# A recurrence's filler products cut into smaller parts, and vector steps put in another order, in a two-block transformer kernel

## The chip, the core and the metric

The kernel runs on one core of a Trainium2 chip. The core has a matrix engine (TensorE, in the rows PE, with PEld for its weight loads), a vector engine (VectorE, DVE), a scalar engine (ScalarE, ACT), GpSimd (POOL) and SyncE (SP, here the one that streams weights in). The engines run their own instruction lists and wait for one another through semaphores. The metric is the device time of one execution in microseconds, lower is better.

## What is computed

The reference runs two blocks over 512 tokens of 1024 values in float32. The change touches the first block; its mixer holds the recurrence (HGRN2, four heads of 128 keys, both directions) around which most of the change lies:

```python
def forget(z, lb):
    f = lb + (1.0 - lb) * jax.nn.sigmoid(z.astype(f32))
    return ((1.0 - f)..., jnp.log(f)...)
k_f, lf_f = forget(fz_f, lb_fwd)
k_b, lf_b = forget(fz_b, lb_bwd)
o_f = gla_chunkwise(qh, k_f, lf_f, vh)           # S_t = diag(f_t) S_{t-1} + k_t v_t^T, o_t = S_t^T q_t
o_b = gla_chunkwise(qh[:, ::-1], k_b[:, ::-1], lf_b[:, ::-1], vh[:, ::-1])[:, ::-1]
...
def first_block(...):
        h = h + token_mixers(rms_norm(h, norm_mix[l]), ...)
        h = h + memory_cross_attention(rms_norm(h, norm_mem[l]), rms_norm(mem, norm_mem_kv[l]), ...)
        h = h + conv_ffn(rms_norm(h, norm_ffn[l]), ...)
    return rms_norm(h, final_norm)
```

The second block (two attentions, with a top-k selection) is left as it was.

## The kernel before

**Products.** Every float32 product is made of three matmuls on rounded halves: high times high (line 621), low times high (622), high times low (623). A group of the three is called a *triple* here; a projection of 128 output columns over 1024 inputs is 8 triples of 512 columns. Weights come as slots of 128x1024 from one long stream: SyncE loads a slot into `ring` (2 deep), GpSimd splits it into `wH` and `wL` (3 deep; lines 573, 574, 576), and signals `split_done`. TensorE opens slots in stream order, so the list `STREAM` and the order of the products must agree. Products land in two PSUM banks in turn (slot number modulo 2), and a bank is opened again when the engine that reads it has freed it.

**The recurrence.** A head has four tiles of 128 tokens (`ST`). For each head h, TensorE turns the logarithms of the forget gates (`turn_logs`, line 756), sums them to decays between tiles (`cross_decays`, 746 and 747) and inside one (`tile_decays`, 788), which ScalarE exponentiates into `E` (`decays`, 1383). VectorE multiplies `E` by queries and keys into `X` (`tile`, 1933; `cross`, 1887 to 1894), TensorE makes scores of `X` in `pair[3]` (`tile_scores`, 801 to 806), VectorE multiplies them by level masks into `lev` (1942) and adds the levels up into `Sg` (1948); these two together are `select`. `output` (836) takes `Sg` to the values. There is one `lev` and one `pair[3]`: `tile_scores` of a tile waits for the masks of the tile before (`masked`), and the mask waits for the sum of the levels before (`s_made`).

Ahead of head h+1 VectorE makes its gates (`forget`, 1858 and 1859, into `lf`), ScalarE their logarithm (1365), TensorE `turn_logs(h+1)`, ScalarE the high part (`logs_high`, 1369), VectorE the low part (`logs_low`, 1953, into `lftL`), for which `cross_decays(h+1)` waits. `keys` (1864, 1867) scales the keys in place.

**The filler.** Between these dependent steps TensorE projects what comes later: while head h runs, the four products and the value turn of head h+2 (`beside(h, j)`, in heads 2 and 3 the attention's q, k, v and the gate), whole products but for one, which `half_step` cuts into 4 and 4 triples around `tile_scores(h, 3)` and `cross_decays(h+1)`.

**The norms.** After the products `mix_out` and `mem_o`, VectorE takes each of 8 chunks (`residual`, 1823), scales it (`with_gain`, 2229), subtracts ScalarE's rounded high part for `nL` of the chunk before (`low`, 1757), and adds the chunk's square to `sums` (`accumulate`, 1766). The next product reads `nL` chunk by chunk; one matmul over `sums` (606) follows.

The order on each engine is the order in which its block of the program is written.

Of the kernel before, what the change touches and what calls it, by code (L numbers as in the profile page):

```python
# [23 lines left out]
P = 128  # L24
# [40 lines left out]
SPL = 3  # L65
# [13 lines left out]
for _h in (1, 2):  # L79
# [6 lines left out]
    ("head2", [1] * 3 + [0]), ("head3", [1] * 4 + [0]), ("q_a", [1] * 4),  # L86
# [31 lines left out]
def head_at(h, j):  # L118

    if j == 0 and h in (1, 2):  # L120
        return f"forget{h}", 0
    if j == 4 and h < 2:
        return f"turn{h}", 0
    return f"head{h}", j - (h in (1, 2))
# [144 lines left out]
def build(nc, stream, xT, memT, pos, vecs, ident_d, const_r, const_a, const_d, sink_d, relb_d, gvec, x1_d, out_d):  # L269
    with ExitStack() as ctx:  # L270
# [318 lines left out]
        def _(pe):  # L589
# [126 lines left out]
            def half_step(h, half):  # L716

                g = head_slot(h, 3)
                if half == 0:
                    open_bank(g)  # L720
                    open_slot()
                r = (n_slot[0] - 1) % SPL
                for k in range(4 * half, 4 * half + 4):
                    last = three(bank(g % 2), weight(r, k), n_parts[k], k == 0, k == DC - 1)
                if half:
                    last.then_inc(multiplied, 1)
# [15 lines left out]
            def recurrence(beside):  # L742
# [109 lines left out]
                for h in range(HG_HEADS):  # L852
# [6 lines left out]
                    tile_scores(h, 1)  # L859
                    if more:  # L860
                        beside(h, 2)
                    else:
                        project("v_a", 0, 1, n_parts)
# [4 lines left out]
                    if h + 2 < HG_HEADS:  # L868
                        half_step(h + 2, 0)
                    else:  # L870
                        beside(h, 3 if more else 2)
                    tile_scores(h, 3)
                    if more:
                        cross_decays(h + 1)
                    if h + 2 < HG_HEADS:
                        half_step(h + 2, 1)
                    if not more:
                        beside(h, 3)
                    if more:
                        tile_decays(h + 1, 0)  # L880
                    beside(h, 4)
                    if more:
# [133 lines left out]
            def head_beside(h, j):  # L1016
                if h + 2 < HG_HEADS:
                    head_step(h + 2, j)
                elif h + 2 == HG_HEADS and j < 4:
                    project("q_a", j, 1, n_parts)  # L1020
                elif h + 1 == HG_HEADS:
                    if j == 1:
                        project("k_a", 0, 1, n_parts)
                    if j < 2:
                        for c in (2 * j, 2 * j + 1):
                            rotate("first", c, qa[:, c, :], FIRST["q_a"] + c, c_a("perm", 0, P), q_turn(c))
# [238 lines left out]
        def _(act):  # L1265
# [94 lines left out]
            def recurrence(beside):  # L1360
# [52 lines left out]
                for h in range(HG_HEADS):  # L1413
                    n, more = UNITS * h, h + 1 < HG_HEADS
                    cross_copies(h)
                    decays(n + 2, LQ)
                    beside(h, 1)
                    decays(n + 3, LQ)
                    if more:
                        logs(h + 1)  # L1420
                    decays(n + 4, LQ)
                    beside(h, 2)
                    if more:
                        logs_high(h + 1)
# [1218 lines left out]
```

## Time and profile before

| what | value |
|---|---|
| time before, median of 3 runs (range) | 1480.76 us (1479.05 to 1482.13) |
| the profiled execution, its own time | 1481.16 us |
| its span, first to last instruction | 1479.4 us |
| TensorE matmuls busy | 1454.1 us, 98% of the span |
| VectorE / ScalarE / GpSimd busy | 928.5 / 452.5 / 832.8 us |
| mean granted TensorE clock | 0.997 |

The profiled execution's time is 1.76 us more than its span; the sums of the prediction are made against this execution. "Busy" of TensorE counts modelled ends of pipelined matmuls that overlap, so what is left of the span is what it stood still, by a lower bound.

### The profile page before, as it was taken

What the parts mean: (1) busy time and instruction counts of PE and PEld (TensorE: products, weight loads), DVE (VectorE), ACT (ScalarE), POOL (GpSimd) and SP (SyncE); (2) the same over time, 40 slices, a digit from 0 to 9 for tenths busy, and PEclk for the clock granted to TensorE, in tenths of its full rate; (3) what the DMA queues carried; (4) which work ended last, traced back from release to release, by engine and by line L of the source; (5) the groups of instructions that cost most, each with busy time, mean ns of one, the idle gap of its engine ahead of it and who ended that gap; (6) DMA issues with size and microseconds to landing.
All of it is one profiled execution on the core that took longest, in us unless ns stands there. A gap on an engine that the chain in (4) does not pass through costs nothing.

```text
span 1479.4 us, 20094 instructions
## 1 busy us (share of the span) xinstructions
PE 1454.1 (98%) x7044; PEld 1151.7 (78%) x7044; DVE 928.5 (63%) x1685; ACT 452.5 (31%) x889; POOL 832.8 (56%) x675
## 2 busy tenths in 40 slices
PE   9999999999999999999999999999999999999998
PEld 7877777767788888778888888887867677767887
DVE  5577787787238433478777673334877777696245
ACT  4456332376123122320101001112343334464112
POOL 5624313534566777466776767766665354444662
PEclk9999999999999999999999999999999999999999
DMA  5311112121333333233333333334324542323332
GB/s 197 87 57 58 41 31 58 57 61 55 114 100 100 114 101 109 64 99 88 97 100 100 92 94 103 110 100 137 99 72 146 93 104 57 114 72 108 106 93 78
DMA packets 37017, 135.60 MB, mean 92 GB/s; under 512 B 4296, under 2 KB 4552, under 8 KB 36296
## 3 DMA queue, kind: packets, MB, share of 16 engines
q1 hardware_dynamic: 33264, 121.13, 27.3%
q10 hardware_dynamic: 3672, 13.35, 3.5%
q8 instruction: 56, 0.92, 0.2%
q14 instruction: 25, 0.20, 0.0%
HBM read 127.64 MB, written 6.82 MB: 91 GB/s over the span
## 4 chain that ended last, share of the span: by engine, by line
PE 88%; DVE 6%; issue 2%; ACT 2%; PEld 1%; DMA 0%; PEldq 0%; DVEq 0%; ACTq 0%
PE pair L621 25%; PE pair L623 24%; PE pair L622 24%; PE pair L908 4%; PE pair L936 3%; PE pair L920 2%; PE pair L836 1%; PE pair L788 1%; PE pair L801 1%; DVE X L1933 1%; DVE dx L2089 1%; PE pair L705 0%; PE pair L823 0%; DVE selm L2365 0%; DVE dx L2086 0%
## 5 line engine op out<-in xcount | busy, mean ns | idle before, releaser
L576 POOL TENSOR_TENSOR wL<-ring,wH 128x1024 fp32r<-128x1024 f32 x223 | 546.9, 2453 | 18.6
L621 PE MATMUL pair<-nH,wH 128*128 128x512 f32 x1064 | 426.3, 401 | 3.2 <-DVE nL L1757 1.9
L623 PE MATMUL pair<-nH,wL 128*128 128x512 f32 x1064 | 414.9, 390 | 0.0
L622 PE MATMUL pair<-nL,wH 128*128 128x512 f32 x1064 | 414.7, 390 | 0.0
L573 POOL TENSOR_TENSOR tick<-tick 128x1 f32<-128x1 f32 x223 | 57.5, 258 | 604.3 <-PE pair L623 558.0
L621 PEld LDWEIGHTS pair<-nH,wH 128*128 128x128 f32 x1064 | 199.7, 188 | 64.3 <-issue 18.9
L574 POOL TENSOR_SCALAR wH<-ring 128x1024 fp32r<-128x1024 f32 x223 | 237.1, 1063 | 0.0
L623 PEld LDWEIGHTS pair<-nH,wL 128*128 128x128 f32 x1064 | 199.7, 188 | 42.7
L622 PEld LDWEIGHTS pair<-nL,wH 128*128 128x128 f32 x1064 | 199.9, 188 | 41.2 <-issue 1.9
L1600 ACT ACTIVATE sgb<-cv 128x512 f32<-128x512 f32 x22 | 13.9, 634 | 209.5 <-DVE cv L2274 209.5
L621 PE MATMUL pair<-aH,wH 128*128 128x512 f32 x176 | 68.5, 389 | 0.0
L622 PE MATMUL pair<-aL,wH 128*128 128x512 f32 x176 | 68.5, 389 | 0.0
L623 PE MATMUL pair<-aH,wL 128*128 128x512 f32 x176 | 68.5, 389 | 0.0
L1766 DVE TENSOR_TENSOR sums<-sums,sq 128x512 f32<-128x512 f32 (+1 forms) x30 | 53.0, 1766 | 11.7 <-ACT sq L1298 11.0
L1933 DVE TENSOR_TENSOR X<-E,qT 128x128 f32<-128x128 f32 x96 | 31.7, 331 | 44.8 <-ACT E L1383 44.8
L2273 DVE SCALAR_TENSOR_TENSOR cv<-gpad,vec,cv 128x512 f32<-128x512 f32 x22 | 56.7, 2579 | 0.8
L2300 DVE TENSOR_TENSOR hT<-pair,hT 128x512 f32<-128x512 f32 x8 | 5.5, 692 | 77.3 <-PE pair L623 77.3
L1457 ACT ACTIVATE dx<-dx,stat 128x128 f32<-128x128 f32 (+3 forms) x64 | 36.0, 563 | 55.9 <-DVE stat L2095 55.6
L2270 DVE TENSOR_TENSOR gpad<-pair,rstd 128x512 f32<-128x512 f32 x22 | 15.2, 692 | 56.3 <-PE pair L623 56.2
L2107 DVE TENSOR_SCALAR dx<-dx,stat 128x128 f32<-128x128 f32 (+3 forms) x64 | 45.9, 717 | 2.3
L1383 ACT ACTIVATE E<-pair 128x768 f32<-128x768 f32 (+1 forms) x40 | 32.0, 853 | 40.8 <-PE pair L747 23.5
L621 PEld LDWEIGHTS pair<-aH,wH 128*128 128x128 f32 x176 | 33.0, 188 | 6.9
(403 smaller groups left out, 2657.6 us busy)
## 6 DMA issues: line engine op xcount, KB each, us to landing
ring<-stream SPq DMA_DIRECT2D x223, 512.0 KB, 3.6
gvec<-gv ACTq DMA_DIRECT2D x1, 2560.0 KB
hT<-xT SPq DMA_DIRECT2D x4, 512.0 KB, 6.0
x_d<-hT ACTq DMA_DIRECT2D x1, 2048.0 KB, 7.3
toep<-gvec ACTq DMA_DIRECT2D x8, 256.0 KB, 3.3
hT<-x_d ACTq DMA_DIRECT2D x1, 2048.0 KB, 8.6
out<-yo SPq DMA_DIRECT2D x4, 512.0 KB, 3.6
cD<-const_d ACTq DMA_DIRECT2D x1, 1345.0 KB, 6.4
```

What stands on the lines that cost most here:

```text
L573: pool.tensor_tensor(tick[:, 1:2], tick[:, 0:1], tick[:, 0:1], ALU.add).then_inc(high_done, 1)
L574: pool.tensor_scalar(high, ring[:, r, :], 1.0, 0.0, ALU.mult, ALU.add).then_inc(high_done, 1)
L576: pool.tensor_tensor(low, ring[:, r, :], high.bitcast(F32), ALU.subtract).then_inc(split_done, 1)
L621: mm(out, a[0], b[0], start=first, stop=False)
L622: mm(out, a[0], b[1], start=False, stop=False)
L623: return mm(out, a[1], b[0], start=False, stop=last)
L908: last = mm(out, *pairs[t], start=t == 0, stop=t == count - 1)
L936: last = mm(out[rows, qs], w, turned[:, j % 2, t, qs], start=n_t == 0, stop=n_t == len(kind["serves"]) - 1)
L1766: V.tensor_tensor(sums[:, :width], sums[:, :width], sq[:, a % 2, :width], ALU.add).then_inc(sq_added, 1)
L1933: last = V.tensor_tensor(out, factors(kind), src, ALU.mult)
L2107: V.tensor_scalar(px, px, st[:, 5:6], None, ALU.mult).then_inc(a_prob, 1)
L2273: own(V.scalar_tensor_tensor(out=y, in0=x[:, 0:S], scalar=w[0], in1=y, op0=ALU.mult, op1=ALU.add))
```

## The change

It has four parts. (1) TensorE's filler is cut at triples: `beside_part(h, j, a, b)` issues triples a to b of a product. In heads 0 and 1 the groups between recurrence steps were 8, 8, 4, 4, 8 triples and are 8, 6, 6, 2, 4, 6; in head 2 they were 8, 8, 8 and are 8, 6, 5, 2, 3. The first product of the next head (`forget3`, `q_first`) begins before the value turn, so the stream's order changes there. (2) VectorE makes the gates and scaled keys of head h+1 before tile 1 of head h (for head 0 the scaled keys directly behind its gates), and ScalarE takes their logarithm behind the exponentials of tile 1. (3) `select` is cut into `masks` and `levels`, and the masks of tile 1 go ahead of the products of tile 2. (4) In the two residual norms, the low part of the last chunk goes ahead of the last addition to `sums`, and an addition is made before the next chunk's product is taken.

```diff
@@ -83,7 +83,7 @@
     ("head0", [1] * 4), ("forget1", [1]), ("turn0", [0]), ("head1", [1] * 3), ("forget2", [1]), ("turn1", [0]),
-    ("head2", [1] * 3 + [0]), ("head3", [1] * 4 + [0]), ("q_a", [1] * 4),
+    ("head2", [1] * 3), ("forget3", [1]), ("turn2", [0]), ("head3", [1] * 3), ("q_first", [1]), ("turn3", [0]), ("q_a", [1] * 3),
     ("q_turn", [0] * 2), ("k_a", [1]), ("q_turn2", [0] * 2), ("v_a", [1]), ("g_first", [1]),
@@ -117,11 +117,16 @@
-    if j == 0 and h in (1, 2):
+    if j == 0 and h:
         return f"forget{h}", 0
-    if j == 4 and h < 2:
+    if j == 4:
         return f"turn{h}", 0
-    return f"head{h}", j - (h in (1, 2))
+    return f"head{h}", j - (h > 0)
+def q_at(c):
+    return ("q_a", c - 1) if c else ("q_first", 0)
@@ -713,17 +718,11 @@
-            def half_step(h, half):
-                g = head_slot(h, 3)
-                if half == 0:
-                    open_bank(g)
-                    open_slot()
-                r = (n_slot[0] - 1) % SPL
-                for k in range(4 * half, 4 * half + 4):
-                    last = three(bank(g % 2), weight(r, k), n_parts[k], k == 0, k == DC - 1)
-                if half:
-                    last.then_inc(multiplied, 1)
+            def beside_part(h, j, a, b):
+                stage, c = head_at(h + 2, j) if h + 2 < HG_HEADS else q_at(j)
+                project_part(FIRST[stage] + c, n_parts, a, b)
@@ -857,29 +856,33 @@
                     tile_scores(h, 1)
+                    cuts = (4, 6) if h + 2 < HG_HEADS else (3, 5)
                     if more:
-                        beside(h, 2)
+                        beside_part(h, 2, 0, 6)
                     else:
...
                         turn_logs(h + 1)
-                    if h + 2 < HG_HEADS:
-                        half_step(h + 2, 0)
+                        beside_part(h, 2, 6, DC)
+                        beside_part(h, 3, 0, cuts[0])
                     else:
-                        beside(h, 3 if more else 2)
+                        beside(h, 2)
                     tile_scores(h, 3)
                     if more:
+                        beside_part(h, 3, *cuts)
                         cross_decays(h + 1)
+                        beside_part(h, 3, cuts[1], DC)
+                        if h + 2 < HG_HEADS:
+                            beside_part(h + 1, 0, 0, 2)
+                        tile_decays(h + 1, 0)
+                    else:
+                        beside(h, 3)
+                    beside(h, 4)
                     if h + 2 < HG_HEADS:
-                        half_step(h + 2, 1)
-                    if not more:
-                        beside(h, 3)
-                    if more:
-                        tile_decays(h + 1, 0)
-                    beside(h, 4)
-                    if more:
+                        beside_part(h + 1, 0, 2, DC)
+                    elif more:
                         beside(h + 1, 0)
@@ -1017,13 +1020,13 @@
                 elif h + 2 == HG_HEADS and j < 4:
-                    project("q_a", j, 1, n_parts)
+                    project(*q_at(j), 1, n_parts)
                 elif h + 1 == HG_HEADS:
...
                         for c in (2 * j, 2 * j + 1):
-                            rotate("first", c, qa[:, c, :], FIRST["q_a"] + c, c_a("perm", 0, P), q_turn(c))
+                            rotate("first", c, qa[:, c, :], FIRST[q_at(c)[0]] + q_at(c)[1], c_a("perm", 0, P), q_turn(c))
                     elif j == 2:
@@ -1414,14 +1417,15 @@
                     decays(n + 2, LQ)
+                    if more:
+                        logs(h + 1)
                     beside(h, 1)
                     decays(n + 3, LQ)
+                    decays(n + 4, LQ)
                     if more:
-                        logs(h + 1)
-                    decays(n + 4, LQ)
+                        logs_high(h + 1)
                     beside(h, 2)
                     if more:
-                        logs_high(h + 1)
                         decays(n + UNITS, S)
@@ -1819,11 +1823,11 @@
                 for c in chunks:
+                    if c >= 2:
+                        accumulate(name, c - 1)
                     b, free = product(stage, c)
...
                     after(c)
-                    if c >= 2:
-                        accumulate(name, c - 1)
                 if DC - 1 in chunks:
@@ -1858,10 +1862,13 @@
-                def keys(h):
+                def scaled_keys(h):
...
                         own(V.tensor_scalar(kk[:, d, h, :], kk[:, d, h, :], lb(2, d, h), lb(1, d, h), ALU.mult, ALU.add))
+                def key_sums(h):
                     if h:
@@ -1942,7 +1949,10 @@
                                     ALU.mult).then_inc(masked, 1)
-                    dve.wait_ge(masked, m + 1)
+                def levels(h, i):
+                    dve.wait_ge(masked, ST * h + i + 1)
                     if h and i == 0:
@@ -1962,13 +1972,14 @@
                 def start(h):
-                    keys(h)
+                    key_sums(h)
                     out_of_bank(dve, head_slot(h, 2))
...
                 forget(0)
+                scaled_keys(0)
                 queries(0)
@@ -1988,22 +1999,28 @@
                             turn_queries(c)
+                    if more:
+                        dve.wait_ge(x_made, UNITS * h + 2)
+                        forget(h + 1)
+                        scaled_keys(h + 1)
                     tile(h, 1)
-                    select(h, 0)
-                    if more:
-                        forget(h + 1)
-                    else:
+                    masks(h, 0)
+                    levels(h, 0)
+                    if not more:
                         turn_queries(2)
                         turn_queries(3)
+                    masks(h, 1)
                     tile(h, 2)
-                    select(h, 1)
+                    levels(h, 1)
                     tile(h, 3)
-                    select(h, 2)
+                    masks(h, 2)
+                    levels(h, 2)
                     if more:
...
                         queries(h + 2)
-                    select(h, 3)
+                    masks(h, 3)
+                    levels(h, 3)
                     if more:
@@ -2229,6 +2246,8 @@
                         low(name, c - 1, nH, nL)
+                    if c == DC - 1:
+                        low(name, c, nH, nL)
                 return use
@@ -2237,7 +2256,6 @@
             residual("mix_out", "mem", range(2, DC), scale_queries)
-            low("mem", DC - 1, nH, nL)
             own(V.memset(nomask[:, :], 0.0))
```

The weights' host arrays are cut to the new stream names accordingly; `q_at` is also used where q is rotated and copied out.

**TensorE, head 0 to head 1.** The first place is where head 0's last scores (lines 801 to 806, in the change 800 to 805) are followed by the decays between tiles of head 1 (746 and 747, in the change 745 and 746). Before:

```order
L801 MATMUL pair<-X 128x128 [waits masked,x_made]
L801 MATMUL pair<-X 128x128 x5
L805 MATMUL pair<-xq,xk 128x128
L806 MATMUL pair<-qT,kfb 128x128
L746 MATMUL pair<-cR,lftH 128x256 [waits lft_made]
L747 MATMUL pair<-cR,lftL 128x256
```

In the change (626 to 628 are the three matmuls of a triple):

```order
L800 MATMUL pair<-X 128x128 [waits masked,x_made]
L800 MATMUL pair<-X 128x128 x5
L804 MATMUL pair<-xq,xk 128x128
L805 MATMUL pair<-qT,kfb 128x128
L626 MATMUL pair<-nH,wH 128x512
L627 MATMUL pair<-nL,wH 128x512
L628 MATMUL pair<-nH,wL 128x512
L626 MATMUL pair<-nH,wH 128x512
L627 MATMUL pair<-nL,wH 128x512
L628 MATMUL pair<-nH,wL 128x512
L745 MATMUL pair<-cR,lftH 128x256 [waits lft_made]
L746 MATMUL pair<-cR,lftL 128x256
```

Two triples now stand between the scores and the matmul that waits for `lft_made`. The second place is the end of the decays between tiles in head 2, where the decays of head 3's first tile wait for ScalarE's exponentials. Before:

```order
L746 MATMUL pair<-cR,lftH 128x128
L747 MATMUL pair<-cR,lftL 128x128
L788 MATMUL pair<-cR,lftH 128x384 [waits exp_done]
L788 MATMUL pair<-cR,lftH 128x384
L788 MATMUL pair<-cR,lftL 128x384 x2
```

In the change:

```order
L745 MATMUL pair<-cR,lftH 128x128
L746 MATMUL pair<-cR,lftL 128x128
L626 MATMUL pair<-nH,wH 128x512
L627 MATMUL pair<-nL,wH 128x512
L628 MATMUL pair<-nH,wL 128x512
L626 MATMUL pair<-nH,wH 128x512
L627 MATMUL pair<-nL,wH 128x512
L628 MATMUL pair<-nH,wL 128x512
L626 MATMUL pair<-nH,wH 128x512
L627 MATMUL pair<-nL,wH 128x512
L628 MATMUL pair<-nH,wL 128x512
L787 MATMUL pair<-cR,lftH 128x384 [waits exp_done]
```

Three triples have come in between.

**VectorE, ahead of the recurrence.** The place is behind head 0's gates (`lf`), with its queries (`qT`), the constants' cast (`cR`) and the first steps of the rotary angles (`ang`). Before:

```order
L1859 TENSOR_SCALAR lf<-lf 128x1024 [waits dve_own]
L1961 SCALAR_TENSOR_TENSOR qT<-pair,sgb 128x512 [waits multiplied,sg_made]
L1974 CAST cR<-landing 128x1408 [waits ld_r]
L2043 CAST ang<-posi 128x32 [waits ld_pos]
L2044 TENSOR_SCALAR ang<-ang,vec 128x32 [waits dve_own]
```

In the change:

```order
L1863 TENSOR_SCALAR lf<-lf 128x1024 [waits dve_own]
L1868 TENSOR_SCALAR kk<-kk,lbs 128x512
L1868 TENSOR_SCALAR kk<-kk,lbs 128x512 [waits dve_own]
L1971 SCALAR_TENSOR_TENSOR qT<-pair,sgb 128x512 [waits multiplied,sg_made,dve_own]
L1985 CAST cR<-landing 128x1408 [waits ld_r]
```

The two scalings of the keys now stand ahead of the queries and of all that follows up to `logs_low(0)`; they stood behind it before.

## Rows read from the trace of the kernel before

**Rows 1.** The page, part 1: busy time, share of the span, instructions.

```profile
PE 1454.1 (98%) x7044; PEld 1151.7 (78%) x7044; DVE 928.5 (63%) x1685; ACT 452.5 (31%) x889; POOL 832.8 (56%) x675
```

**Rows 2.** Waits of TensorE between 40 and 265 us: total, times, longest.

```profile
PE pair L788 <- ACT E L1383: 2.0, 1, 2.0
PE pair L746 <- DVE lftL L1953: 2.0, 2, 1.0
PE pair L801 <- DVE lev L1942: 1.8, 2, 1.0
```

**Rows 3.** Timeline of TensorE in head 0: start, us; in brackets idle before, releaser.

```profile
88.62 0.48 PE L621 MATMUL pair<-nH,wH 128*128 128x512 f32 x1
...
94.29 0.44 PE L788 MATMUL pair<-cR,lftH 64*128 64x384 f32 x2
...
101.81 1.57 PE L801 MATMUL pair<-X 128*128 128x128 f32 x12 [0.95 <-DVE lev L1942]
...
104.81 0.39 PE L746 MATMUL pair<-cR,lftH 128*128 128x256 f32 x1 [0.97 <-DVE lftL L1953]
...
107.67 0.45 PE L621 MATMUL pair<-nH,wH 128*128 128x512 f32 x1
...
110.56 0.44 PE L788 MATMUL pair<-cR,lftH 64*128 64x384 f32 x2
```

**Rows 4.** The chain that ended last: start, us, what; rotations (705) and outputs (836).

```profile
163.74 3.43 PE pair L836 x8
...
203.43 3.30 PE pair L705 x4
206.72 3.75 PE pair L836 x8
...
221.60 1.88 PE pair L705 x4
```

**Rows 5.** A window of head 2: PE, PEld, DVE, ACT, POOL busy, granted clock, DMA.

```profile
204.00:206.00 2.00, 2.00 (x4) 0.97 (x3) 2.00 (x7) 0.98 (x2) 0.00 (x0) 0.50 0.00 0
```

**Rows 6.** Timeline of VectorE in head 0.

```profile
82.18 0.29 DVE L1933 TENSOR_TENSOR X<-E,qT 128x128 f32<-128x128 f32 x1 [17.24 <-ACT E L1383]
...
84.61 1.22 DVE L1942 TENSOR_TENSOR lev<-pair,cA 128x1024 f32<-128x1024 f32 x1
85.86 1.99 DVE L1948 TENSOR_REDUCE Sg<-lev 128x128 f32<-128x1024 f32 x1
87.77 2.90 DVE L1858 TENSOR_SCALAR lf<-kk,lbs 128x512 f32<-128x512 f32 x2
```

**Rows 7.** Timeline of ScalarE in head 2: the exponentials of `cross_decays(3)`.

```profile
200.47 1.94 ACT L1383 ACTIVATE E<-pair 128x1024 f32<-128x1024 f32 x2 [8.99 <-PE pair L747]
```

**Rows 8.** Timelines of GpSimd, VectorE and TensorE ahead of the recurrence.

```profile
33.58 2.72 POOL L576 TENSOR_TENSOR wL<-ring,wH 128x1024 fp32r<-128x1024 f32 x1
...
35.43 0.69 DVE L1961 SCALAR_TENSOR_TENSOR qT<-pair,sgb 128x512 f32<-128x512 f32 x1 [1.39 <-ACT sgb L1354]
...
38.40 2.25 DVE L2046 TENSOR_SCALAR turn<-ang 128x32 f32<-128x32 f32 x1
...
44.91 1.22 DVE L1953 TENSOR_TENSOR lftL<-pair,lftH 128x1024 fp32r<-128x1024 f32 x1
...
46.74 0.36 PE L746 MATMUL pair<-cR,lftH 128*128 128x256 f32 x1
```

**Rows 9.** Timeline of VectorE: the two key scalings, with GpSimd idle.

```profile
108.43 1.12 DVE L1864 TENSOR_SCALAR kk<-kk,lbs 128x512 f32<-128x512 f32 x2
```

**Rows 10.** Timelines at the two residual norms: TensorE's waits, VectorE.

```profile
490.43 1.13 PE L606 MATMUL pair<-sums,ones 128*128 128x512 f32 x2 [0.31 <-DVE sums L1766]
...
661.84 0.50 PE L621 MATMUL pair<-nH,wH 128*128 128x512 f32 x1 [1.08 <-DVE nL L1757]
...
658.09 3.08 DVE L1766 TENSOR_TENSOR sums<-sums,sq 128x512 f32<-128x512 f32 x2
661.10 0.69 DVE L1757 TENSOR_TENSOR nL<-pair,nH 128x512 fp32r<-128x512 f32 x1
```

More of the change, by code:

```diff
@@ L1539, in head_beside @@
                 elif h + 2 == HG_HEADS and j < 4:
-                    copy_out("q_a", j, qa[:, j, :])
+                    copy_out(*q_at(j), qa[:, j, :])
                 elif h + 1 == HG_HEADS and j == 1:
@@ L1934, in tile, with masks @@
                     last.then_inc(x_made, 1)
-                def select(h, i):
+                def masks(h, i):
                     m = ST * h + i
@@ L2258, in _ @@
             residual("mem_o", "ffn", after=with_gain("mem_o", "ffn", "norm_ffn"))
-            low("ffn", DC - 1, nH, nL)
             V.tensor_tensor(g12[:, :], vec[:, VEC["final_norm"]:VEC["final_norm"] + DC],
@@ L2569, in weight_stream @@
         "g_first": blocks(g_r[:, :P]), "g_rest": blocks(g_r[:, P:]),
-        "q_a": blocks(q_a), "k_a": blocks(k_a), "v_a": blocks(v_a),
+        "q_first": blocks(q_a[:, :P]), "q_a": blocks(q_a[:, P:]), "k_a": blocks(k_a), "v_a": blocks(v_a),
         "rec_mix": mixed(gate_r, a["w_br_rec"][0]), "att_mix": mixed(gate_a, br_att),
@@ L2585, in weight_stream @@
         four = np.concatenate([blocks(w[:, cs]) for w in (fz_f, fz_b, q_r, i_r)], 0)
-        if h in (1, 2):
+        if h:
             parts[f"forget{h}"], four = four[:1], four[1:]
```

## The prediction, written before the result was known

> **What bounds the kernel now.** I read the page first: TensorE's matmuls are busy 98% of the span [rows 1]. The change removes no matmul, so it can only win time in which TensorE stands still or runs slowly, and lose by making more of it. The view of waits of TensorE over the recurrence (40 to 265 us) gives what is there to win: 2.0 us once for ScalarE's exponentials, 2.0 in two waits for `lftL`, 1.8 in two waits for the masks `lev` [rows 2]. The timeline shows the place of one pair, in head 0: 0.95 us ahead of the scores of tile 3, at 101.81, and 0.97 ahead of `cross_decays(1)`, at 104.81 [rows 3]; the other pair is head 1's. The 2.0 us wait is head 2's, at the end of the exponentials that run from 200.47 to 202.41 [rows 7].
>
> That last wait has a second price. Behind it the granted clock is 0.50 in the window from 204 to 206 us, the lower of the two levels (1.2 against 2.4 GHz), with TensorE busy all through [rows 5]. In the chain, the two rotations there take 3.30 us against 1.88 for two others later, and the output 3.75 against 3.43 in the head before [rows 4]: 1.42 + 0.32 = 1.74 us. What TensorE did before it fell is 2 us of standing still; behind the waits of about 1 us in head 0 the triples keep their pace (4 from 107.67 to 110.56, [rows 3]).
>
> Outside, two waits belong to the residual norms: 0.31 us for `sums` at 490.43, and 1.08 us for `nL`'s last chunk at 661.84 [rows 10].
>
> **What VectorE does to the head's waits.** In head 0 VectorE is idle 17.24 us ahead of the products of tile 1, and then runs tile 1 (82.18 to 84.61, 2.43 us), masks 1.22, levels 1.99 and the two gate steps 2.90 in a row [rows 6], with the gates' lower bound behind. So the gates of head 1 sit in the middle of the chain that TensorE waits for at 101.81, while room is free in front of it.
>
> **Part 1 and 2, heads 0 and 1.** I redo the chain with the change's order, on the clock of before. TensorE begins its filler at 88.62, so the scores of tile 1 are made. A triple is (94.29 - 88.62) / 8 = 0.71 us [rows 3]. VectorE: masks of tile 1 at 88.9 to 90.1, products of tile 2 to 92.6. TensorE: six triples to 92.9, then the decays of tile 3, and only then the scores of tile 2, so these don't wait. `turn_logs(1)` waits for ScalarE's exponentials of tile 3 as before, with the same work between the two, and comes two triples (1.4 us) sooner. The products of tile 3 need those exponentials. Taken as ready by 95.7, the latest that fits, the products end at 98.1, the masks of tile 2 at 99.4, the levels at 101.4, `logs_low(1)` (1.22, [rows 8]) at 102.6. TensorE comes to the scores of tile 3 at 101.81 - 0.95 = 100.9 (needs 99.4), and to `cross_decays(1)` at 104.81 - 0.97 - 0.95 + 1.42 = 104.3 (needs 102.6). Both waits go, with 1.5 and 1.7 us to spare. The four triples behind `cross_decays(1)` stay, and cover its exponentials as before. The value turn needs the raw values copied out, which now come two triples behind `cross_decays(1)` instead of four, so this is nothing new. The bank that `forget3` takes ahead of the turn is freed by the queries of head 2, which VectorE makes right behind `logs_low(1)`, before TensorE has even ended `cross_decays(1)`.
>
> Win: 2.0 + 1.8 = 3.8 us for both heads. Cost: one more change between filler and other matmuls in each. Four triples took 2.89, eight 5.67 [rows 3], so a cut costs 2 x 2.89 - 5.67 = 0.11; both heads 0.2.
>
> The gates with the scaled keys (2.90 and 1.12, [rows 6, 9], and the gates' lower bound, under 5 us in all) now lie in the 17 us gap in head 0. In heads 1 and 2 the gap was not read row by row here; tiles 1 start a like time behind the outputs, and I take it as room enough. ScalarE's logarithm moves with them and needs no engine that is late.
>
> **Head 2.** Three triples behind `cross_decays(3)` are 2.1 us, against exponentials of 1.94 with a hand-over each side [rows 7]: just covered. Its scores of tile 3 come five triples behind `turn_logs`, not eight: 2.1 us sooner, and the forward chain of VectorE has lost the gates, 2.90 us and more, so no wait by the same sum. Win 2.0, and with the standstill the slow stretch, 1.74; cost two cuts more, 0.2. Net 3.5. If the clock falls all the same, 1.8.
>
> **Part 3, ahead of the recurrence.** This one costs. The two key scalings need 1.12 us with GpSimd idle [rows 9], and VectorE has 1.39 us idle ahead of head 0's queries at 35.43, so alone they would be free. But GpSimd's low split stands from 33.58 to 36.30 there, and a scaling beside such a split does not run: at 38.40 a VectorE step of 32 columns took 2.25 us [rows 8]. So the scalings run from 36.3 to 37.4, the queries (which read PSUM) end at 38.1 instead of 36.1, and the steps behind them up to `logs_low(0)` are about 1.9 us late. That `lftL` was ready at 46.13, TensorE took it at 46.74 [rows 8]: 0.6 to spare, so a new wait of 1.3 us. From both sides: 0, if the later steps lose less beside GpSimd's later passes; 3.3, if one more low split (2.0 of the 2.25) falls on them. I take 1.3, because the lateness is close to the length of one such block and the splits there follow one another. A standstill of 1.3 is nearer to the 0.95 that left the clock alone than to the 2.0 that did not.
>
> The Trainium skill, "SBUF — State Buffer", section "Who interferes with whom", has a rule that speaks against this step: a VectorE instruction in a two-port mode, such as a scaling in SBUF, and a GpSimd one exclude each other, and the second to issue stands until the first has ended. By the rule the 1.3 stays in the sum; without it the scalings fit the 1.39 and the sum is 1.3 better. The trace agrees, with the 2.25.
>
> **Part 4, the norms.** In the second norm `nL`'s last chunk (0.69) stood behind two additions of 3.08 together; ahead of them it can start near 658.1 and end at 658.8, against 661.84 - 1.08 = 660.8 at which TensorE wants it [rows 10]. Win 1.08. What is late next is `sums`, with one addition instead of two behind it, and a whole product (5.67) ahead of its matmul: hidden. In the first norm one addition instead of two: win 0.31.
>
> **Head 3.** The masks of tile 1 (1.22) go ahead of the products of tile 2, which makes these 1.22 later. TensorE has a whole product there as before; I cost it at 0, and at up to 0.5 if the cover just fails.
>
> **Sum.** -3.8 + 0.2 - 3.5 + 1.3 - 1.4 = -7.2 us. On the profiled execution: 1481.16 - 7.2 = 1474.0. The median of the runs is 0.4 lower than that execution, 1480.76, which gives 1473.6; I say 1473.7.
>
> **Rivals.**
> - *The clock falls in head 2 all the same.* For it: the small matmuls around are the same. Against it: three triples stand in the gap. It gives 1473.7 + 1.7 = 1475.4. Chance 0.11.
> - *The waits of heads 0 and 1 only move.* VectorE loses none of its work, and each of its steps can be held by a GpSimd pass (2.25 for 32 columns, [rows 8]). If one holds it in each of heads 0 and 1, the 1.5 spare is gone and most of the 3.8 comes back: 1477.5, and for half of this case above 1477.8. Chance 0.10.
> - *The wait ahead of the recurrence is long.* At its upper end of 3.3: 1475.7. Chance 0.05.
> - *The change gives nothing*: what is won is given back in waits behind the recurrence. No row speaks for it; 1480. Chance 0.04.
> - *Slower: GpSimd's splits come late.* VectorE's gates hold GpSimd at each head's start, TensorE then waits for `split_done`. A split starts when a slot is used up and is wanted two groups later, 11.3 us on; its low half lasts 2.72 [rows 8] and the high half no longer, so about 6 us are spare. The gates and keys, under 5 us, don't reach that. It begins to cost from 6 us of holding on, and loses over the whole from (7.2 + 3) / 3 = 3.4 us more in each of three heads, thus 9.4 us each; the time is then 1484. Chance 0.04.
>
> **How the numbers follow.** The forecast has the rest, 0.66, its own range 1471.5 to 1476: the bounds of part 3 (0 to 3.3 against 1.3), and the scatter of the runs of about 1.5. The whole range, 1471.0 to 1477.5, takes in the first and third rival and about half of the second. A measurement of this kernel tells about 0.2%, 3.0 us, from no change. Faster by more (under 1477.8): 0.66 + 0.11 + 0.05 + 0.05 = 0.87; within: 0.05 + 0.04 = 0.09; slower: 0.04.
>
> **What would show it.** In the waits of TensorE the rows for `lev`, `lftL` and the exponentials in heads 0 to 2 are gone, and one of 1 to 1.5 us for `lftL` stands ahead of `cross_decays(0)`; the clock in the window behind head 2's `cross_decays(3)` is 1.00, and its two rotations take 1.9. No wait for `nL` ahead of `up`, none for `sums` in the first norm. VectorE's gates lie in its long gap. It is wrong if the waits stand elsewhere in the heads, if the first wait is over 2 us and draws the clock down, or if TensorE waits for `split_done`.

## The result, and the profile after

| | before | after |
|---|---|---|
| median of the runs beside one another (range) | 1480.8 us (1477.4 to 1482.26, 6 runs) | 1471.28 us (1471.13 to 1473.98, 6 runs) |
| the profiled execution, its span | 1481.16, 1479.4 us | 1471.64, 1469.8 us |
| TensorE matmuls busy | 1454.1 us, 98% | 1451.5 us, 99% |
| mean granted TensorE clock | 0.997 | 0.998 |

The changed kernel is faster: the ratio is 0.9943, 95% interval 0.9928 to 0.9958. A second series gave 1471.19 against 1480.6 us, 0.9938 (0.9921 to 0.9955). One timed run of the experiments below, of head 2 without its cover, took 2617.18 us at a mean clock of 0.743 and is left out of its numbers.

The page's part 1 after the change, to be laid beside [rows 1]:

```profile
PE 1451.5 (99%) x7044; PEld 1150.7 (78%) x7044; DVE 931.6 (63%) x1685; ACT 450.3 (31%) x887; POOL 833.7 (57%) x675
```

The number of matmuls is the same, 7044; only standstill and slow time went. Next, TensorE's waits over the recurrence in the changed kernel (20 to 265 us; in total, times, longest), for [rows 2]:

```profile
PE pair L731 <- ACT kk L1441: 0.7, 1, 0.7
PE pair L710 <- ACT gr L1289: 0.3, 1, 0.3
PE pair L745 <- DVE lftL L1963: 0.3, 1, 0.3
PE pair L800 <- DVE X L1940: 0.2, 1, 0.2
```

The 5.8 us for the exponentials, `lftL` and `lev` are gone. The first two rows stand in the kernel before as well, with 0.7 and 0.3, in and behind head 3. Two small ones are new: 0.3 for `lftL` ahead of the recurrence, and 0.2 for `X` at the first scores of head 3. (Line numbers are up to 17 higher than in the kernel before, some 1 lower.) Now TensorE's timeline in head 0 (start, us), for [rows 3]:

```profile
89.14 0.48 PE L626 MATMUL pair<-nH,wH 128*128 128x512 f32 x1
...
93.43 0.44 PE L787 MATMUL pair<-cR,lftH 64*128 64x384 f32 x2
...
101.00 0.39 PE L628 MATMUL pair<-nH,wL 128*128 128x512 f32 x1
101.22 1.50 PE L800 MATMUL pair<-X 128*128 128x128 f32 x12
...
104.38 0.28 PE L745 MATMUL pair<-cR,lftH 128*128 128x256 f32 x1
```

There is no bracket ahead of the scores at 101.22 or of `cross_decays(1)` at 104.38. The prediction had 100.9 and 104.3. What VectorE does meanwhile in the changed kernel, for [rows 6]:

```profile
65.34 3.07 DVE L1862 TENSOR_SCALAR lf<-kk,lbs 128x512 f32<-128x512 f32 x2
...
69.05 2.02 DVE L1868 TENSOR_SCALAR kk<-kk,lbs 128x512 f32<-128x512 f32 x2
82.73 0.30 DVE L1940 TENSOR_TENSOR X<-E,qT 128x128 f32<-128x128 f32 x1 [11.66 <-ACT E L1386]
...
95.99 0.30 DVE L1940 TENSOR_TENSOR X<-E,qT 128x128 f32<-128x128 f32 x1 [1.06 <-ACT E L1386]
...
98.43 1.22 DVE L1949 TENSOR_TENSOR lev<-pair,cA 128x1024 f32<-128x1024 f32 x1
...
101.62 1.21 DVE L1963 TENSOR_TENSOR lftL<-pair,lftH 128x1024 fp32r<-128x1024 f32 x1
```

The gates and keys (65.34 to 71.07) take their time out of the gap, which shrinks from 17.24 to 11.66 us. The masks of tile 2 end at 99.65 and `lftL` at 102.83, 1.6 us before TensorE wants each (99.4 and 102.6 were predicted). In the kernel before, the low clock of [rows 5] lay on head 2's two rotations and outputs. In the changed kernel that work comes some 6 us earlier, and the windows that hold it show the full clock:

```profile
196.00:198.00 2.00, 2.00 (x12) 1.14 (x11) 1.78 (x3) 1.52 (x4) 1.66 (x2) 1.00 0.02 4
198.00:200.00 2.00, 2.00 (x6) 0.87 (x5) 2.00 (x2) 0.71 (x2) 1.92 (x2) 1.00 0.00 0
```

And the timeline of TensorE in head 2, where the rotations (now L710) and outputs (L835) of [rows 4] took 3.30 and 3.75:

```profile
197.10 1.98 PE L710 MATMUL pair<-qa,cA 128*128 128x512 f32 x4
198.92 3.61 PE L835 MATMUL pair<-Sg,vr 128*128 128x512 f32 x8
...
205.34 0.94 PE L800 MATMUL pair<-X 128*128 128x128 f32 x6 [0.19 <-DVE X L1940]
```

**Where the 9.6 us of the span went.** Landmarks in TensorE's timeline are each head's first matmul over `E` (its scores across tiles; before at 74.73, 120.88, 167.01 and 210.31 us), the last head's first output, the first turn of `wx`, the two norm sums, and the memory product `mk` by `mq`. The time between two is a stage. The last two columns are a further execution of each kernel, from the series below, in which head 2 had no low clock.

| stage | before | after | before, again | after, again |
|---|---|---|---|---|
| values' turn to head 0's scores over `E` | 28.35 | 28.90 | 28.35 | 28.91 |
| to head 1's | 46.15 | 43.76 | 46.14 | 43.69 |
| to head 2's | 46.13 | 43.77 | 46.06 | 43.77 |
| to head 3's | 43.30 | 39.63 | 41.62 | 39.62 |
| to the last head's output | 41.57 | 41.75 | 41.43 | 41.69 |
| output to the first turn of `wx` | 40.33 | 40.45 | 38.74 | 40.46 |
| to the first norm's sum | 198.22 | 197.72 | 198.10 | 197.71 |
| to the memory product | 12.92 | 12.80 | 12.91 | 12.81 |
| to the second norm's sum | 159.28 | 157.93 | 159.29 | 157.92 |

The first two columns differ by 0.55 - 2.39 - 2.36 - 3.67 + 0.18 + 0.12 - 0.50 - 0.12 - 1.35 = -9.54 us. The 38.74 in the third column, against 40.3 to 40.5 in the others of its row, is the stage without a low clock near 250 us: two such places come and go between executions, head 2 in the kernel before and this one in both kernels.

### The profile page after: what moved, and what is told of

It reads as the page before. It is cut to its first block, busy times and chain, and to the rows that moved or that the text cites. A ratio compares the mean times of both kernels' runs of the same rounds, so it can differ in the third digit from the quotient of the medians.

```text
span 1469.8 us, 20093 instructions
## 1 busy us (share of the span) xinstructions
PE 1451.5 (99%) x7044; PEld 1150.7 (78%) x7044; DVE 931.6 (63%) x1685; ACT 450.3 (31%) x887; POOL 833.7 (57%) x675
## 4 chain that ended last, share of the span: by engine, by line
PE 89%; DVE 6%; issue 1%; ACT 1%; PEld 1%; DMA 0%; PEldq 0%; DVEq 0%; ACTq 0%
PE pair L626 25%; PE pair L628 24%; PE pair L627 24%; PE pair L911 4%; PE pair L939 3%; PE pair L923 2%; PE pair L800 1%; PE pair L787 1%; PE pair L835 1%; DVE dx L2106 1%; DVE selm L2382 0%; DVE dx L2103 0%; PE pair L746 0%; PE pair L745 0%; PE pair L822 0%
## 5 line engine op out<-in xcount | busy, mean ns | idle before, releaser
L1940 DVE TENSOR_TENSOR X<-E,qT 128x128 f32<-128x128 f32 x96 | 28.7, 299 | 25.6 <-ACT E L1386 25.5
```

## The experiments

Theory: each part works as the prediction's chain reckons it, and what is left is prices. Rival: the stalls are not won by the parts named; the gain is the clock's, or one part's alone. Medians are of the runs of one series. Where a series' own median of before is given, it is the one beside these runs.

**The norms alone.** Only part 4 of the diff, in the kernel before.

```diff
+                    if c >= 2:
+                        accumulate(name, c - 1)
...
+                    if c == DC - 1:
+                        low(name, c, nH, nL)
```

> The kernel before with part 4 alone (last low part ahead of the last addition, additions one chunk ahead). Theory: a wait costs its idle row and about 0.25 us more, since the idle is counted from the modelled end of the last matmul, so the landmarks behind the first norm come 0.5 us sooner and behind the second another 1.3: together -1.8 us. Rival: a wait costs its row alone: -0.31 and -1.08, together -1.4 us, and the rest of the surplus over the forecast lies elsewhere.

Measured: 1479.55 us (1476.98 to 1481.11, 12 runs) against 1478.97 (29 runs); 0.9999 (0.9989 to 1.0009). By the medians that is no change, and the interval just leaves out a gain of 2 us. But the medians mix clocks: of the 51 runs of before beside the experiments 17 show a mean clock of 0.999 or 1.000, of these 12 none. At a like mean clock, 0.996, five of its runs have a median of 1479.74 and ten of before 1481.76: 2.0 us less. The stages say the same: its norms take 197.71, 12.80 and 157.93 us, those of the changed kernel, and all of its stages in heads 0 to 2 are those of the kernel before. So part 4 is worth 0.50 + 0.12 + 1.35 = 2.0 us (1.9 against the second execution of before), the theory's 1.8 and not the rival's 1.4, and stands apart from the rest. In the changed kernel's timeline of VectorE the last chunk's low part stands directly behind the one before (two in one row), ahead of the sums:

```profile
649.24 1.45 DVE L1761 TENSOR_TENSOR nL<-pair,nH 128x512 fp32r<-128x512 f32 x2
650.61 1.52 DVE L1770 TENSOR_TENSOR sums<-sums,sq 128x512 f32<-128x512 f32 x1
```

**The cuts alone.** The filler and the stream of the changed kernel, with VectorE's, ScalarE's and the norms' order of before.

```diff
-                        beside(h, 2)
+                        beside_part(h, 2, 0, 6)
...
+                        beside_part(h, 2, 6, DC)
+                        beside_part(h, 3, 0, cuts[0])
```

> The kernel before with the filler cuts of TensorE alone (and logs_high ahead of the second copy, which the cuts need); gates, masks and norms as before. Theory: in heads 0 and 1 the gates still stand in VectorE's chain, so the 0.95 us wait for lev stays and only the wait for lftL (0.97) is covered by the two triples ahead of cross_decays: -1.2 us a head; in head 2 the three triples behind cross_decays cover the exponentials and the clock stays at 1.00: -3.7 us. Sum -6.1 us, about 1474.7. Rival: the order of VectorE is what counts and the cuts alone only move the waits: under -3 us.

Measured: 1476.22 us (1474.54 to 1479.21, 12 runs), 0.9974 (0.9963 to 0.9985). The waits for `lftL` and for the exponentials are gone, but the wait for `lev` is in three heads and 1.2 each (TensorE's waits, 20 to 265 us):

```profile
PE pair L800 <- DVE lev L1949: 3.6, 3, 1.2
```

The cause is in VectorE's timeline of head 0:

```profile
90.14 2.91 DVE L1862 TENSOR_SCALAR lf<-kk,lbs 128x512 f32<-128x512 f32 x2
93.09 0.69 DVE L1863 TENSOR_SCALAR lf<-lf 128x1024 f32<-128x1024 f32 x1
...
96.13 1.22 DVE L1949 TENSOR_TENSOR lev<-pair,cA 128x1024 f32<-128x1024 f32 x1
```

and in TensorE's:

```profile
97.49 1.58 PE L800 MATMUL pair<-X 128*128 128x128 f32 x12 [1.24 <-DVE lev L1949]
```

The gates stand ahead of the masks of tile 1, while TensorE now wants the bank for tile 2 two triples sooner, 1.24 us before it gets it at 97.49. Heads 0 and 1 win 1.2 us each, as the theory had it, though the wait for `lev` has moved from tile 3 to tile 2. Head 2 has one too, which the theory missed: its stage takes 40.89 us, where the whole change has 39.63. So the cuts win 2.75 us by the medians, not 6.1, and inside the rival's "under 3".

**The orders alone.** Parts 2 and 3, with the filler uncut.

```diff
+                        dve.wait_ge(x_made, UNITS * h + 2)
                         forget(h + 1)
-                    else:
+                        scaled_keys(h + 1)
+                    tile(h, 1)
```

> The kernel before with VectorE's and ScalarE's new order alone (gates and scaled keys early, masks of tile 1 ahead), TensorE's filler uncut, norms as before. Theory: both waits of heads 0 and 1 go, -2.4 us a head with the 0.25 behind each; head 2 keeps its 2.0 us wait for the exponentials and the clock falls behind it as before, 0; ahead of the recurrence +0.6. Sum -4.2 us, about 1476.6. Rival: without the cuts the waits stay, since TensorE gets to them no later: -1 us or less.

Measured: 1479.59 us (1477.76 to 1482.28, 12 runs), 1.0005 (0.9994 to 1.0017). The rival's number came, not the theory's -4.2. Heads 0 and 1 take 46.16 and 46.10 us, as before, the stage ahead of them 28.93, as in the changed kernel, and all the waits stand:

```profile
PE pair L751 <- DVE lftL L1964: 2.3, 3, 1.0
PE pair L793 <- ACT E L1388: 2.0, 1, 2.0
PE pair L806 <- DVE lev L1950: 1.8, 2, 0.9
```

VectorE is early now, and waits for the exponentials of tile 3 instead, which follow TensorE's decays behind eight uncut triples:

```profile
98.72 1.46 DVE L1941 TENSOR_TENSOR X<-E,qT 128x128 f32<-128x128 f32 x1 [2.39 <-ACT E L1388]
```

So in heads 0 and 1 the cuts alone win 2.4 us, the orders alone nothing, both together 4.75. The loop between TensorE and VectorE has two limits, and each half of the change lifts one.

**Scaled keys of head 0 behind its queries.** The changed kernel with this one line back in its place.

```diff
-                scaled_keys(0)
                 ...
+                scaled_keys(0)
```

> The changed kernel with the scaled keys of head 0 put back behind the rotary angles. Theory: the wait of 0.33 us for lftL ahead of cross_decays(0) goes and 0.25 behind it: 0.6 us less than the changed kernel, with the landmark of head 0's first turn back at 74.3 us. Rival: the 0.48 us by which head 0 starts later comes from elsewhere (the first norm's waits differ by 0.4 us twice in the two traces), and nothing moves.

Measured: 1470.74 us (1468.89 to 1473.33, 6 runs), 0.5 us under the changed kernel. The first stage takes 28.33 us instead of 28.90, and the wait for `lftL` at 47.24 is gone. The new order costs 0.57 us. How, VectorE's and GpSimd's timelines of the changed kernel show:

```profile
33.86 3.95 DVE L1868 TENSOR_SCALAR kk<-kk,lbs 128x512 f32<-128x512 f32 x2
37.85 0.69 DVE L1971 SCALAR_TENSOR_TENSOR qT<-pair,sgb 128x512 f32<-128x512 f32 x1
38.46 2.36 DVE L1985 CAST cR<-landing 128x1408 fp32r<-128x1408 f32 x1
...
45.87 1.22 DVE L1963 TENSOR_TENSOR lftL<-pair,lftH 128x1024 fp32r<-128x1024 f32 x1
33.48 2.71 POOL L581 TENSOR_TENSOR wL<-ring,wH 128x1024 fp32r<-128x1024 f32 x1
...
37.62 2.44 POOL L581 TENSOR_TENSOR wL<-ring,wH 128x1024 fp32r<-128x1024 f32 x1
```

The scalings take 3.95 us beside a low split, 1.12 without one [rows 9]. The queries start 2.4 us late (35.43 in [rows 8]), and the cast behind them falls on the next split: it takes 2.36 us, 1.00 with the scalings back in their place, and is 3.8 late at its end. But a few steps on, the on-time chain is held by a third split, and the late one finds GpSimd idle. The same two steps with the scalings behind the queries, and in the changed kernel:

```profile
43.63 2.56 DVE L2068 SCALAR_TENSOR_TENSOR rest<-turn,rest 128x64 f32<-128x64 f32 x2
```

```profile
45.18 0.48 DVE L2068 SCALAR_TENSOR_TENSOR rest<-turn,rest 128x64 f32<-128x64 f32 x2
```

`lftL` starts at 45.87, against 44.91 [rows 8]: 0.96 late, not 1.9. The Trainium skill, "SBUF — State Buffer", section "Who interferes with whom", says that of a VectorE instruction in a two-port mode, which a cast can be, and a GpSimd one, the one that issues first has the shared pair of ports for its whole instruction, and the other stands. The trace agrees: the cast issued 0.84 us behind the split and ended 0.8 us behind the split's end.

**Changed kernel again.**

> The changed kernel once more, beside the other three. The structural gain is put at 7.7 us against the kernel before at a like mean clock; so 1471.3 is expected at a mean clock of 0.998, and about 1.7 us more or less for each stretch at half clock more or less. Rival: the 9.5 us between the first medians is all the change's own; then the difference of the medians is again 9 to 10 us.

Measured: 1471.19 us (1469.54 to 1473.82, 6 runs) against 1480.6 (11 runs), 0.9938 (0.9921 to 0.9955). Its runs stand on levels: 1469.5 to 1469.6 at a mean clock of 1.000, 1471.1 to 1471.3 at 0.998, 1473.8 at 0.996. Before has such levels as well: of 57 runs in all series, 17 lie between 1477.22 and 1477.53 and the median is 1480.6. Lowest level against lowest level the change wins 7.8 us, median against median 9.4. Both descriptions of the expectation hold a part: 7.8 is the order's, the rest is the clock's.

**Head 2 without its cover.** All triples ahead of `cross_decays(3)`, none behind it.

```diff
-                    cuts = (4, 6) if h + 2 < HG_HEADS else (3, 5)
+                    cuts = (4, 6) if h + 2 < HG_HEADS else (3, 8)
```

> The changed kernel with all five last triples of head 2's product ahead of cross_decays(3), none behind it. Both theories expect the wait for the exponentials again, 1.9 to 2.1 us near 204 us. Theory A (the clock falls because TensorE stood still there): the granted clock falls to 0.5 behind it in every run, and the kernel is 3.5 to 4.0 us slower than the changed one. Theory B (the low stretch comes at this place in some executions and not in others): it costs the wait alone, 1.8 to 2.2 us, and a profile shows a fall there or not.

> The version with the 2.0 us wait of head 2 brought back, once more, for one profile. Theory A: a low stretch near 206 us. Theory B: in some executions only; the stage takes 41.6 us without one and 43.3 with one.

Measured: five runs of 1471.37 to 1474.22 us, and 1477.62 once more on its own. The median of the five, 1472.81, is 1.6 us over that of the changed kernel, the lowest 1.8 over its lowest: theory B's price, not the 3.5 to 4.0 of theory A. In the first profile the wait of 2.03 us is back and the clock stays; head 2's stage takes 41.64 us. In the second the same wait is there and the clock falls; the stage takes 44.65. TensorE's timeline and windows of that second execution:

```profile
199.54 0.69 PE L787 MATMUL pair<-cR,lftH 64*128 64x384 f32 x2 [2.03 <-ACT E L1387]
```

```profile
197.00:198.00 1.00, 0.52 (x5) 0.37 (x4) 0.00 (x0) 0.45 (x1) 1.00 (x1) 1.00 0.00 0
198.00:199.00 1.00, 0.00 (x0) 0.00 (x0) 0.00 (x0) 1.00 (x2) 0.90 (x1) 1.00 0.00 0
199.00:200.00 1.00, 0.46 (x2) 0.46 (x4) 0.41 (x1) 0.98 (x2) 0.00 (x0) 0.52 0.00 0
200.00:202.00 2.00, 2.00 (x9) 1.18 (x8) 2.00 (x5) 0.77 (x2) 0.00 (x0) 0.50 0.85 256
```

The first execution, in the window that holds its wait and the one behind:

```profile
197.00:198.00 1.00, 0.00 (x0) 0.00 (x0) 0.00 (x0) 1.00 (x2) 0.57 (x1) 1.00 0.00 0
198.00:199.00 1.00, 0.81 (x8) 0.65 (x8) 0.76 (x2) 0.63 (x2) 0.00 (x0) 1.00 0.72 66
```

In the second, the clock falls while TensorE still stands, in the last of the 2 us, and stays at 0.50 though TensorE is busy again. So the cover is worth 2.0 us in both, and up to 3.0 more in some executions.

**The kernel before, once more.**

> The kernel before once more, for one profile: is there a low stretch behind the 2.0 us wait near 204 us? Theory A (it follows the standstill always): yes. Theory B (a standstill makes it possible, and it comes in some executions only): either; with none of it the execution is about 1.7 us shorter, and the step from the scores of head 2 to those of head 3 takes 41.6 rather than 43.3 us.

Measured: 1479.01 us. The same wait of 2.03 us stands at 203.84, and behind it (windows):

```profile
202.00:204.00 2.00, 0.15 (x2) 0.16 (x4) 1.93 (x5) 2.00 (x3) 0.00 (x0) 1.00 0.76 236
204.00:206.00 2.00, 2.00 (x11) 1.17 (x12) 2.00 (x5) 1.43 (x3) 0.00 (x0) 1.00 0.08 31
```

No fall; the stage takes 41.62 us, not 43.30. Of the fourteen profiled executions of this study, six have the wait (before twice, the norms alone, the orders alone, head 2 without its cover twice) and three of these show a low clock there; eight don't have it, and none of them does. Three low clocks scattered by chance over fourteen would all fall on those six once in 18 times, so that the wait brings the fall is likely and not certain.

**Masks of tile 1 behind the products again**, in all heads.

```diff
-                    masks(h, 1)
                     tile(h, 2)
+                    masks(h, 1)
```

> The changed kernel with the masks of tile 1 behind the products of tile 2 again, in all heads. Theory A (moving them was needed, as the chain of lev reckons it): the wait for lev ahead of the scores of tile 2 appears in heads 0 to 2, where that tile's scores now come after six triples rather than eight, 0.3 to 1.2 us each, so 1 to 3 us slower. Theory B (the other two parts make room enough): no wait, and 0.2 us faster since the 0.19 us wait for X in head 3 goes.

Measured: 1471.1 us (1469.39 to 1471.32, 6 runs). No wait for `lev`; heads 0 to 2 take 43.76, 43.70 and 39.61 us. The third part of the diff is worth nothing here. But the wait for `X` ahead of head 3's scores stays too (0.18), so the moved masks didn't make it, against theory B. What does: it stands in all eight profiled executions whose head 2 has no 2 us wait, and that stage takes 41.7 to 41.8 us; it is in none of the six with the wait, and there the stage takes 41.4 to 41.6. TensorE arrives 2 us sooner, and up to 0.3 of it is given back where VectorE's products are next late.

**The token sums.** Near 250 us there is a second low stretch in some executions. In the changed kernel's second execution it begins in the outputs behind a row of one-column matmuls; TensorE isn't idle there (timeline, then windows):

```profile
241.83 2.15 PE L731 MATMUL pair<-ones,kk 128*128 128x1 f32 x18
243.84 2.50 PE L835 MATMUL pair<-Sg,vr 128*128 128x512 f32 x4
```

```profile
244.00:246.00 2.00, 2.00 (x4) 0.83 (x5) 1.73 (x7) 0.18 (x1) 1.19 (x1) 0.78 0.00 0
246.00:248.00 2.00, 2.00 (x4) 0.82 (x3) 1.43 (x8) 0.00 (x0) 0.00 (x0) 0.50 0.71 217
```

One version spreads twelve of them between the triples of the product beside them, in three last changes with the scaled keys of head 0 and the last head's masks of tile 1 back in their places; the control has the two other changes and leaves the row.

```diff
+                for k in range(DC):
+                    project_part(FIRST["g_rest"], n_parts, k, k + 1)
+                    for n in range(3 * k // 2, 3 * (k + 1) // 2):
+                        hd, i = tiles[n]
+                        last = mm(bank(3)[:, n:n + 1], kk[:, 0, hd, P * i:P * i + P], ones[:, 0:1], ...)
```

> The changed kernel with the scaled keys of head 0 behind its queries (worth 0.5 us by the earlier run), the last head's masks of tile 1 behind its products (0.2 us), and the last head's 12 one-column token sums spread between the triples of the product beside it instead of standing in one row. Theory A (the half clock near 250 us comes of the row of one-column matmuls): the stretch is gone in each profile, 1.7 us, so 1468.8 to 1469.2, 2.3 us under the changed kernel. Theory B (it comes and goes with the execution): 1470.5 to 1470.8, only the 0.7 us, with a low stretch near 250 us in some executions as before.

> The spread version once more, beside its control. Theory A: again at least 4 of 6 runs at 1469.0 to 1469.3, no low stretch near 250 us in the profile, median 1.5 us under the control. Theory B: its runs fall on the levels as the control's do, medians within 0.5 us.

> The control for the spread sums: scaled keys of head 0 behind its queries, the last head's masks of tile 1 behind its products, and the 12 one-column token sums in one row as in the changed kernel. At a mean clock of 1.0 it should equal the spread version, 1468.9 to 1469.2, by both theories. Theory A (the low stretch near 250 us comes of the row): most runs lie one stretch higher, 1470.4 to 1470.9, and at most 2 of 6 at the lowest level. Theory B (it comes and goes whatever the order): its runs fall on the levels as those of the spread version do, about 4 of 6 at the lowest.

Measured: spread 1469.19 us (1468.96 to 1471.41, 6 runs; 0.9927, 0.9912 to 0.9942) and 1469.95 (1469.04 to 1471.68, 6 runs; 0.993, 0.9915 to 0.9945). Control 1471.88 (1469.01 to 1473.61, 6 runs; 0.9938, 0.9921 to 0.9955). Both reach the same lowest level, so the spread itself costs and wins nothing at full clock. Beside one another the control's median lies 1.9 us over the spread version's, near theory A's 1.5. On the lowest level lie 7 of 12 runs of the spread version, and 2 of 6 of the control; together with the changed kernel and the two other variants that keep the row and have no 2 us wait, 6 of 30 lie on their lowest level. A low stretch near 250 us is in 7 of 12 profiled executions with the row and in neither of the two without. It points to the row, and 18 runs beside one another don't settle it.

## Why the prediction was right

It said 1473.7 (1471.0 to 1477.5) and the runs gave 1471.28, near the lower end: faster, and for the reasons given, but by 9.5 us where it had 7.2. Head 2's clock isn't what was missed: without its 1.74 the sum is 5.5 us, and the lowest levels of the two kernels lie 7.8 apart, which is the same 2.3 us more. By its terms, from the stages of the two profiled executions:

| term | predicted | measured |
|---|---|---|
| heads 0 and 1, waits less the cuts | -3.8 + 0.2 | -4.75 |
| head 2 | -3.5 | -3.67 |
| head 3, and the stage behind it | 0 | +0.30 |
| ahead of the recurrence | +1.3 | +0.55 |
| norms | -1.4 | -1.97 |
| sum | -7.2 | -9.54 |

- **The chain of head 0** came as it was worked out: every time within 0.5 us, both margins 1.6 (1.5 and 1.7 predicted). The rival of waits that only move falls.
- **The price of a wait was too low.** The sum took the idle time in the row, 0.95 and 0.97. This is the matmul ahead of the scores of tile 3 in the kernel before:

```profile
100.48 0.39 PE L623 MATMUL pair<-nH,wL 128*128 128x512 f32 x1
```

  From its start to that of the scores (101.81, [rows 3]) are 1.33 us; in the changed kernel, 101.00 to 101.22, 0.22. With the slower scores behind the wait (1.57 and 1.50 for the group, 1.42 and 1.34 to the next) it cost 1.2, and the second, 1.36 from start to start (0.14 where there is no wait, in head 2) and 0.1 in its first matmul, about 1.3. Together 2.5, less the cut of 0.1, gives the 2.4 per head. The same shows in the second norm: a row of 1.08, a stage shorter by 1.35. At 1.2 us in the heads and 0.6 in the norms, this is most of what was mis-sized.
- **Head 2**: the sum fits this pair of executions, and its parts do, 2.0 and 1.7. But the clock's part isn't in each execution of the kernel before. "That last wait has a second price" holds in three of six; it is an expectation of the price that belongs in a sum.
- **Ahead of the recurrence** the mechanism was right: the scalings stand beside the split, `lftL` comes late, TensorE waits. The size was taken as one block passed on to the end, and the later splits gave half of it back. It lies within the bounds of 0 to 3.3, but the sign that was named, a row of 1 to 1.5 us for `lftL`, didn't come: the row is 0.33.
- **Head 3** was costed at nothing with the masks as the danger. The masks cost nothing; TensorE's earlier arrival cost 0.2 to 0.3 for `X`.
- **The masks of tile 1**: the prediction's chain had them ahead of the products, and didn't ask if it held without. It does.
- **The other rivals** didn't come either: the clock in head 2 is 1.00, the wait ahead of the recurrence is short, and TensorE waits for GpSimd once in each kernel, for the same 1.0 us near the start, so no split comes late.

The 1.7 us between the difference of the lowest levels (7.8) and that of the medians (9.4) is one low stretch. That it is head 2's is what the profiles point to. How often it falls there in the timed runs, which have no profile by stage, stays open.

## What to carry to other kernels

When two engines pass work back and forth, moving one engine's work earlier is worth nothing if it then waits for the other: reckon the loop with both orders, and expect halves of such a change to measure as a miss (orders alone 1.0005) while the whole doesn't. Price a removed wait of TensorE from start to start against a place where the same two matmuls follow without a wait; the idle row was 0.25 to 0.35 us short. For differences below 0.2% compare stages between landmarks in the trace, since run times here stand on levels 1.5 us and more apart.

## What the hardware showed that was not expected

- The granted clock falls to 0.50 (1.2 of 2.4 GHz) for some 3 to 7 us at a few places of the program (from about 11 to 18 us, head 2, near 250 us), in some executions of the same kernel and not in others. In head 2 and near 250 us such a stretch is worth about 1.7 us (41.62 against 43.30, 38.74 against 40.46), once 3.0. Ahead of it TensorE stood for 2 us in one place, and was busy with one-column matmuls in another.
- Arriving later can cost less: 3.8 us of lateness behind the blocked VectorE steps became 0.96 because the next steps missed a GpSimd split that had held them for 2 us.
- The best version here (scaled keys of head 0 behind the queries, the last head's masks of tile 1 behind its products, sums spread) runs at 1469.2 and 1469.95 us in two series, 1.2 to 2.1 us under the changed kernel's; its control, without the spread, reaches the same lowest level.
